# Visiting order and block sums of 32 experts: from GpSimd on one partition to TensorE and VectorE on 32 partitions

## The reference

```
logits = (tok @ w_router) + b_router           # 288 tokens x 32 experts
top_val, top_idx = lax.top_k(logits, 4)
gate = softmax(top_val)
counts = bincount(flat_e, length=32)           # tokens of each expert
...
hid = xb @ w_e_in[e] + b_e_in[e]               # 1024 x 2048 per expert, float32
act = x_glu * sigmoid(1.702 * x_glu) * (x_lin + 1.0)
out = act @ w_e_out[e] + b_e_out[e]            # 1024 x 1024 per expert, float32
y = sum over a token's 4 experts of gate * out
x = layer_norm(alpha * x + g2 * y, ...)
```

## Time and profile before

| | us |
|---|---|
| median of 3 runs | 1367.17 (1365.32 to 1367.57) |
| the profiled execution | 1369.23 |
| its span, first to last instruction | 1367.5 |
| PE busy | 1095.1 (80%) |
| DVE busy | 509.9 (37%) |
| ACT busy | 173.9 (13%) |
| POOL busy | 84.1 (6%) |
| mean rate of the DMA engines | 334 GB/s |

### The profile page before, as it was taken

One profiled execution on the slowest core, in us unless ns is written; L12 is line 12 of the kernel. 1 busy time (PEld: TensorE's weight loads), 2 busy tenths in 40 slices (PEclk: granted clock), 3 DMA queues, 4 the chain that ended last, 5 costly groups with the idle time before them and its releaser, 6 DMA issues.

```text
span 1367.5 us, 31578 instructions
## 1 busy us (share of the span) xinstructions
PE 1095.1 (80%) x12593; PEld 488.9 (36%) x12594; DVE 509.9 (37%) x1154; ACT 173.9 (13%) x506; POOL 84.1 (6%) x118
## 2 busy tenths in 40 slices
PE   3789888859889999899997997797987887666760
PEld 2556544424324433343433433242423332222210
DVE  0393323854324333243433333233323322222228
ACT  0101222221111111111111111010101100000000
POOL 2700000072000000000000000000000000000003
PEclk9899756969989999899999999898988987878765
DMA  9985851355991798969798999999999999999980
GB/s 327 326 306 193 271 196 62 129 214 214 415 417 61 309 418 335 412 268 418 324 416 323 417 416 416 415 417 417 417 417 417 416 416 416 415 418 417 417 319 35
DMA packets 94555, 457.15 MB, mean 334 GB/s; under 512 B 9163, under 2 KB 16245, under 8 KB 61633
## 3 DMA queue, kind: packets, MB, share of 16 engines
q1 hardware_dynamic: 89984, 450.18, 82.4%
q10 hardware_dynamic: 4481, 5.59, 1.3%
HBM read 452.51 MB, written 3.79 MB: 334 GB/s over the span
## 4 chain that ended last, share of the span: by engine, by line
PE 36%; SPq 30%; DMA 17%; DVE 8%; issue 5%; DVEq 2%; ACT 1%; ACTq 0%; POOL 0%
SPq L373 15%; DMA w<-in_w_e_out 13%; PE bank L1612 13%; SPq L370 9%; PE bank L1639 4%; PE bank L1592 3%; SPq L351 2%; DMA w<-in_w_e_in 2%; PE comb L1571 2%; PE bank L1509 2%; DMA mt<-in_ln_b 1%; SPq L337 1%; DMA w<-in_w_ada 1%; PE comb L1421 1%; PE comb L1418 1%
## 5 line engine op out<-in xcount | busy, mean ns | idle before, releaser
L1612 PE MATMUL bank<-w,mt 128*32 128x512 f32 x3264 | 405.7, 640 | 51.8 <-DMA w<-in_w_e_in 51.8
L1178 DVE TENSOR_TENSOR xy<-comb,xy 128x1024 f32<-128x1024 f32 x156 | 185.2, 1215 | 243.7 <-PE comb L1571 243.7
L1639 PE MATMUL bank<-w,mt 128*32 128x256 f32 x3264 | 204.9, 397 | 49.8 <-DMA w<-in_w_e_out 36.2
L1612 PEld LDWEIGHTS bank<-w,mt 128*32 128x32 f32 x3264 | 96.2, 114 | 320.1 <-issue 207.8
L1215 DVE TENSOR_SCALAR mt<-bank 128x256 f32<-128x256 f32 x51 | 21.6, 424 | 404.9 <-PE bank L1612 404.9
L1639 PEld LDWEIGHTS bank<-w,mt 128*32 128x32 f32 x3264 | 100.7, 113 | 135.7 <-DMA w<-in_w_e_out 53.4
L1592 PE MATMUL bank<-pick,hb 128*128 128x32 bf16 x2448 | 79.4, 179 | 62.3 <-issue 38.2
L1571 PE MATMUL comb<-mt,gpickT 32*128 32x256 f32 (+1 forms) x1248 | 115.9, 456 | 1.9 <-DVE xy L1178 1.4
L1592 PEld LDWEIGHTS bank<-pick,hb 128*128 128x128 bf16 x2448 | 75.1, 98 | 87.4 <-issue 87.4
L803 ACT ACTIVATE mt<-mt 128x256 f32<-128x256 f32 x51 | 21.2, 416 | 513.8 <-DVE mt L1215 513.8
L1593 PE MATMUL bank<-pick,hb 96*128 96x32 bf16 x408 | 72.6, 179 | 0.0
(11 more groups left out here) (320 smaller groups left out, 847.2 us busy)
## 6 DMA issues: line engine op xcount, KB each, us to landing
w<-in_w_e_in SPq DMA_DIRECT2D x256, 1024.0 KB, 20.7
w<-in_w_e_out SPq DMA_DIRECT2D x128, 1024.0 KB, 21.8
w<-in_w_ada SPq DMA_DIRECT2D x12, 2048.0 KB, 11.1
w<-in_w_in SPq DMA_DIRECT2D x3, 2048.0 KB, 22.0
w<-in_w_in SPq DMA_DIRECT2D x2, 1024.0 KB, 21.3
w<-in_w_out SPq DMA_DIRECT2D x4, 512.0 KB, 10.2
w<-in_w_out SPq DMA_DIRECT2D x2, 1024.0 KB, 12.8
w<-mod_rows SPq DMA_DIRECT2D x4, 512.0 KB, 6.4
```

Source lines behind the costliest of these rows:

```text
L1178: return v.tensor_tensor(rows, comb[0:TS[t], :, c:c + 256], rows, ALU.add)
L1612: ins = mm(quarter(bank[0][SLOTS * q:SLOTS * (q + 1), :], 0), xT[:, SLOTS * k:SLOTS * (k + 1)], quarter(slot[s], q), start=False, stop=(k ...
L1639: ins = mm(bank[7][SLOTS * q:SLOTS * (q + 1), 0:256], hid, slot[s][:, D * (k % 2) + 256 * q:D * (k % 2) + 256 * (q + 1)], start=False, sto ...
```

## The change

- PE forms the counts twice, as a column with one expert per partition (`maskb` against a column of ones) and as a row on all 32 partitions (ones against `maskb`), after the ranks instead of before them.
- DVE compares all pairs of experts in one instruction on 32 partitions, with a key of count times 32 plus a tie-breaker, sums each row to a rank, and compares the rank with a constant table `rank_at` of which rank stands at which place. The result `at_place` is a permutation matrix, and `upto` is its running sum along the places.
- PE multiplies the expert numbers with `at_place` and the numbers of blocks with `upto`, in two small matmuls. That gives `order` and the whole of `cum`. DVE copies both to SBUF after the gates, and each copy counts `cum_ready` up by one.
- The constants (`tie`, `tiec`, `rank_at`, `idb`) are written by POOL early in the kernel, ahead of the splitting of the expert biases (L501 to L510). POOL's own work L524 to L562 is gone.
- The rank's two subtractions of 1 (L1159, L1162) are gone; `iota` starts at 1 and `rank` is cleared to 0 in their place.
- PE, ACT and DVE no longer load range ends before expert 0. They enter its loop with 0 and a register that is loaded inside the loop, in each of its blocks: PE behind the last matmul of L1612, ACT behind its second copy of gathered tokens, DVE behind `add_y(0)`. The same place loads expert 1's end.
- SP waits for both copies of `cum_ready` at L415; all waits for `order_ready` are gone.

```
         def opening_range(eng, name):
             return [0] + [eng.alloc_register(f"{name}_end{e}") for e in range(2)]
         def load_ends(eng, ends):
             eng.wait_ge(cum_ready, 2)
             for e in range(2):
                 eng.reg_load(ends[e + 1], cum[0:1, e + 3:e + 4])
...
+            g.iota(idb[:, 0:1], ...)
+            g.iota(tie[:, :], ...)
+            link(g.iota(tiec[:, :], ...))
+            for e, first in ((0, 1e6), (1, 9e5)):
+                link(g.memset(tie[:, e:e + 1], first))
+                link(g.affine_select(out=tiec[:, :], ...))
+            for place, r in enumerate(PLACES):
+                g.memset(rank_at[:, place:place + 1], float(r))
+            link(g.memset(cum[:, 0:3], 0))
+            g.sem_inc(sort_consts, 1)
...
-            dve.wait_ge(cnt_done, 1)                 # DVE L1143 to L1154
-            ... counts, blocks, nblk_ready, cumf, cum, three register loads
             dve.wait_ge(rank_done, 1)
             ... ranks without the two subtractions
+            dve.wait_ge(cnt_done, 1)
+            dve.wait_ge(sort_consts, 1)
+            link(v.tensor_copy(cntc[:, 0:1], bank[7][0:NE, 288:289]))
+            v.scalar_tensor_tensor(out=keyr, in0=bank[7][0:NE, 256:288], scalar=float(NE), in1=tie, op0=MULT, op1=ADD)
+            v.tensor_scalar(over, full, cntc[:, 0:1], None, ALU.is_le)
+            link(v.scalar_tensor_tensor(out=cntc[:, 1:2], in0=cntc[:, 0:1], scalar=float(NE), in1=tiec, ...))
+            link(v.tensor_scalar(keyr, keyr, cntc[:, 1:2], None, ALU.is_gt))
+            v.tensor_reduce(idb[:, 1:2], over, AX_X, ALU.add)
+            link(v.tensor_reduce(cntc[:, 2:3], keyr, AX_X, ALU.add))
+            v.tensor_scalar(idb[:, 1:2], idb[:, 1:2], 1.0, None, ALU.add).then_inc(place_ready, 1)
+            link(v.tensor_scalar(at_place, rank_at, cntc[:, 2:3], None, ALU.is_equal))
+            v.tensor_tensor_scan(upto, at_place, at_place, 0.0, ALU.add, ALU.max).then_inc(place_ready, 1)
             ... gates, seven semaphore increments
+            dve.wait_ge(order_done, 1)
+            v.tensor_copy(cum[:, 3:NE + 3], bank[7][0:1, 352:384]).then_inc(cum_ready, 1)
+            v.tensor_copy(order[:, :], bank[7][0:1, 320:352]).then_inc(cum_ready, 1)
...
+            for t in range(3):                       # PE, behind the ranks
+                mm(bank[7][0:NE, 288:289], maskb[0:TS[t], t, :], ones[0:TS[t], 0:1], ...)
+            for t in range(3):
+                ins = mm(bank[7][0:NE, 256:288], ones[0:TS[t], 0:NE], maskb[0:TS[t], t, :], ...)
+            ins.then_inc(cnt_done, 1)
+            pe.wait_ge(place_ready, 2)
+            mm(bank[7][0:1, 320:352], idb[:, 0:1], at_place[:, :], start=True, stop=True)
+            mm(bank[7][0:1, 352:384], idb[:, 1:2], upto[:, :], start=True, stop=True).then_inc(order_done, 1)
...
-            pe.wait_ge(cum_ready, 1)
...
                     ins.then_inc(m["U"], 1)          # PE, inside the block loop
+                    if isinstance(e, int) and e == 0:
+                        load_ends(pe, ends)
```

More of the change, by code:

```diff
@@ L283, in block_range, with opening_range, load_ends @@
             return lo, hi
+        PLACES = [0, 1] + [31 - (p - 2) // 2 if p % 2 == 0 else 2 + (p - 3) // 2 for p in range(2, NE)]
+        def opening_range(eng, name):
+            return [0] + [eng.alloc_register(f"{name}_end{e}") for e in range(2)]
+        def load_ends(eng, ends):
+            eng.wait_ge(cum_ready, 2)
+            for e in range(2):
+                eng.reg_load(ends[e + 1], cum[0:1, e + 3:e + 4])
         def expert_at(eng, e):
@@ L522, in _ @@
                 g.memset(XY[:, ORD[i], :], 0.0).then_inc(y_zero, 1)
[L524 to L556, removed]
-            link(g.tensor_tensor(grid, across(place), down(ids), ALU.subtract))
-            link(g.tensor_scalar(grid, grid, 0.0, None, ALU.is_le))
-            link(g.tensor_tensor(grid, grid, across(cnt[0:1, 1, :]), ALU.mult))
-            fold(heavy)
-            link(g.tensor_copy(cum[0:1, 5:NE + 3], heavy[:, 2:NE]))
-            g.sem_inc(order_ready, 1)
             pool.wait_ge(ld_x1, 5 * 16)
@@ L1149, in _ @@
-            link(v.tensor_scalar(cnt[0:1, 1, :], cnt[0:1, 1, :], 1.0, None, ALU.add))
-            dve.sem_inc(nblk_ready, 1)
-            link(v.tensor_tensor_scan(cumf[0:1, 3:5], cnt[0:1, 1, 0:2], cnt[0:1, 1, 0:2], 0.0, ALU.add, ALU.max))
-            v.tensor_copy(cum[:, 0:5], cumf[:, 0:5]).then_inc(cum_ready, 1)
-            dve.wait_ge(cum_ready, 1)
-            opening = [block_range(dve, e) for e in range(2)]
             dve.wait_ge(rank_done, 1)
-            link(v.scalar_tensor_tensor(out=rank[:, 0:2, :], in0=bank[1][:, 128:128 + 2 * NE].rearrange("p (t e) -> p t e", t=2), scalar=1.0,
-                                        in1=maskf[:, 0:2, :], op0=ALU.add, op1=ALU.mult))
@@ new lines, in _ @@
+            v.tensor_scalar(over[:, :], full, cntc[:, 0:1], None, ALU.is_le)
+            link(v.scalar_tensor_tensor(out=cntc[:, 1:2], in0=cntc[:, 0:1], scalar=float(NE), in1=tiec[:, :], op0=ALU.mult, op1=ALU.add))
+            link(v.tensor_scalar(keyr[:, :], keyr[:, :], cntc[:, 1:2], None, ALU.is_gt))
+            v.tensor_reduce(idb[:, 1:2], over[:, :], AX_X, ALU.add)
+            link(v.tensor_reduce(cntc[:, 2:3], keyr[:, :], AX_X, ALU.add))
+            v.tensor_scalar(idb[:, 1:2], idb[:, 1:2], 1.0, None, ALU.add).then_inc(place_ready, 1)
@@ L1165, in _ @@
+            link(v.tensor_scalar(at_place[:, :], rank_at[:, :], cntc[:, 2:3], None, ALU.is_equal))
+            v.tensor_tensor_scan(upto[:, :], at_place[:, :], at_place[:, :], 0.0, ALU.add, ALU.max).then_inc(place_ready, 1)
             dve.wait_ge(gexp_done, 3)
@@ L1547, in _ @@
             for t in range(3):
-                ins = mm(bank[2][0:1, 0:NE], ones[0:TS[t], 0:1], maskb[0:TS[t], t, :], start=(t == 0), stop=(t == 2))
-            ins.then_inc(cnt_done, 1)
-            for t in range(3):
                 n = TS[t]
```

64 lines of the change are left out of this document (36 added, 28 removed).

## The result

The changed kernel takes 1360.01 us in the median of 20 runs (1351.88 to 1366.14), the kernel before, timed beside it, 1367.80 us (1362.53 to 1373.56, 20 runs). The ratio is 0.9944 [0.9929, 0.9958]: 7.7 us faster, with 5.7 to 9.7 inside the interval. The forecast was 9.1 us and 1358.1 us; both it and the 6.7 us of rival 1 lie inside the interval, so the times alone can't tell the two apart, and the profiles have to.

The account below looks back on a forecast made before the run. DMA of the experts' weights bounds the kernel, chained to SP's issue at 322.65. 4.3 + 2.66 + 2.42 - 0.3 = 9.1 us off the 1367.17 median gives 1358.1 us, range 1355.0 to 1364.5.

Parts of the forecast that it names:

- rival 1: TensorE's clock falls in the first block's gap all the same: 6.7 us gained, 1360.5 us; chance 0.12.
- A: DVE's path up to expert 0's first block: PE starts at 290.2 instead of 294.47, 4.3 us gained (2.8 to 4.9).
- B: Activation of expert 0's first block, without POOL's work beside it: 2.66 us gained, at least 2.4.
- C: Second product (L1639) of expert 0's first block, at full clock as in the second block: 2.42 us gained (0 to 2.42).
- D: Clock at PE's start, again low after the pause: 0.3 us lost, between 0 and 0.9.
- E: Register loads inside expert 0's loop, hidden behind other work: nothing lost, upper bound 0.8 us.
- F: Work moved and added elsewhere, POOL's early constants and the waits: nothing reaches PE; 2 us if the cover were gone.
- rival 3: PE's jump back misses its code, up to 6.9 us each; chance 0.02 for one, 0.04 for two or more.
- Rival 4: Clock stays low through expert 0: 10.4 us lost against 7.0 gained, 1370.6 us; chance 0.02.
- rival 2: The lead is absorbed where DMA is full in the last third: time stays at 1367; chance 0.07.
- the chain to SP's first issue: Everything after SP's issue at 322.65 is chained to it; a shift there should reach the end one to one.
- The landmark: SP's issue of expert 1's last pieces, at 322.65 before, forecast at 313.5.

Follow-up runs that it names:

- e9: c0 plus 14 dead two-input POOL instructions of 1x1024 from the gather of expert 0's first block on; 1368.95 us in a single execution.
- e1: c0 with POOL's old sort put back as dead work, started once DVE has the numbers of blocks; 1364.89 us (12 runs), ratio to before 0.999.
- e2: c0 with POOL's old sort as dead work, released only after the gather of the first block's tokens; 1358.57 us in a single execution.
- e10: c0 plus ten dead one-input POOL instructions of 1x1024 from the gather of the first block on; 1362.57 us in a single execution.
- e4: c0 plus one dead DVE reduction inside the activation in both blocks of expert 0, POOL silent; 1368.74 us in a single execution.
- e3: c0 with both range ends loaded ahead of expert 0's loop on PE, ACT and DVE; 1367.75 us in a single execution.
- e5: c0 plus 22 dead DVE multiplications, about 10 us, in front of the gates; 1370.65 us (12 runs), ratio to before 1.0031.
- e7: c0 with POOL's three clears of XY moved behind the first block's pick; 1357.70 us (12 runs), ratio to before 0.9923.
- e6: c0 plus 12 dead matmuls of 512 columns while PE waits for DVE before the first block; 0.3 us won to SP's issue.
- e8: e7 plus seven increments moved to POOL, the copies of the sums to ACT, and 19 dead matmuls on PE; 1355.80 us (6 runs), ratio to before 0.9913.
- c0: The changed kernel with each range end loaded with stated bounds, then moved to its register; 1360.58 us (12 runs), ratio to before 0.9955.

## Why the prediction was right

**A, DVE's path (4.3 us, between 2.8 and 4.9): 4.5.** The ten operations took 1.67 us, below my lower bound of 1.7 (2.1 taken): start to start they are 0.16, not 0.21. L1154 took the 0.26 assumed, the two copies 0.59 from start to end (0.35 taken), since 0.22 us of issue lies between them. I missed one thing upstream: `choose` for the last tile took 0.95 us longer in after, because of how L1099 met POOL's clears. In this pair its `lg` began 0.61 earlier, by luck, which hid most of it: measured from the mask, the way to PE shrank by 4.84, and 4.84 - 0.95 + 0.61 = 4.50. So the 4.5 agrees with the 4.3 in part by luck; DVE's path itself beat the sum, mostly in the ten operations (0.5 less) and the gates (0.2 less). The best end, 4.9, is 0.2 more than its terms give: 2.1 less 1.7 is 0.4.

**B, the activation (2.66, at least 2.4): 2.66.** All 51 of these instructions are now alike, where the longest was 2177:

```profile
L1208 DVE SCALAR_TENSOR_TENSOR mt<-mt x51: 425/426/427, 301.7 to 1301.4; 128x256 f32<-128x256 f32 x51
```

Cause shown by e9 and by e1's L1198; e2 shows that the same sort at another time leaves this activation untouched.

**C, the clock in the second product (2.42): 2.42.** Rival 1 is wrong for the first block's gap of 2.77 us; in the same place e10 lost 1.7 us at 3.47, e4 and e9 2.3 and 2.6 at 5.3 to 5.6, so the step stood on 0.7 us at most, which I had not seen. It also stood on a weaker argument than it looked. I took the second block, whose gap of 2.77 left the clock at full, as the model of the first; e4 shows that the second block kept its full clock even behind a gap of 5.30 us, so its rows said little about the first. And TensorE did not stand still for most of the gap before, but for 2.7 of 5.6 us. The result was as forecast; this reason for it was not enough.

**D, the low clock at PE's start (-0.3): -0.18.** It lasted a little over 4 us, as before.

**E, the register loads in the loop (0, at most 0.8): 0.** The line of the loads in the changed kernel, by engine (ns min/median/max, first and last start; all four loads of the two blocks):

```profile
L298 ACTq TENSOR_LOAD <-cum x4: 277/285/478, 291.7 to 309.1; - x4
L298 DVEq TENSOR_LOAD <-cum x4: 305/322/540, 292.9 to 309.8; - x4
L298 PEldq TENSOR_LOAD <-cum x4: 305/312/483, 298.0 to 314.3; - x4
```

PE's sequencer began at 298.0, 2.7 us before the array was through with L1605 (300.69). e3 shows what the move was worth: 1.8 us on the path for two loads, where the prediction removed 2.19 before L1157 for three.

**F, elsewhere (0): 0**, as far as the medians can tell. The five stalls at the jumps back over five experts are all there (6.8 to 7.6 us, at 542.72, 733.76, 864.22, 1029.02 and 1165.97) and no new one of that size, so rival 3 fell; the row of the first, against the earlier trace rows:

```profile
542.72 0.32 PE L1585 MATMUL bank<-pick,hb 128*128 128x32 bf16 x6 [6.98 <-issue]
```

Rival 4 fell with the stretches above (1.00 from 294.5 on), rival 2 with e5. One reading of the page was off: slice 13 of the DMA engines, given as near full, stands at 1. TensorE was busy for 33.0 of the 34 us from 410 to 444 there, so it is work and not a late stream that makes this dip, and the chain to SP's first issue holds.

**The size.** The landmark moved by the 9.1 forecast (9.4 in the pair, 8.8 in the sum of stretches), and the medians by 7.7 with an interval that holds both (and rival 1's 6.7). Where I was too sure was the runs: I took their spread as 2 us from three of them, and it is 11 to 14 over 20.

## What to carry to other kernels

A helper engine that is itself off the critical path can still be paid for there: look at the duration of the same instruction in its other repetitions (median against maximum) before asking whether the helper's work is late. Stretching a gap of a few microseconds in TensorE's work can cost nearly as much again in the clock behind it, and a gap that was safe in one block need not be in another (e4), so the granted clock is worth reading at the very place. In a stream bound by DMA, read a small change at the event that starts the stream, relative to an event ahead of the change; single times of such a kernel say little.

## What was not expected of the hardware

- Beside a POOL instruction with two inputs (1x1024, 1.9 us) a two-input DVE instruction waits to its end, and ends 0.29 us (128x256) or 0.12 us (128x96) after it. Beside a one-input POOL instruction of 2.76 us it was held for 0.7 us, and the next one not at all (e10).
- A DVE `tensor_scalar` of 128x32 took 2.52 us beside three POOL clears of 128x1024 and ended with the last of them (280.13 and 280.10), where it takes 0.23 alone (e7). Before, the same clears were met by three such instructions, at 0.74, 0.89 and 0.41.
- 12 dead matmuls ahead of the first block left its gather at the lower clock (e6); in e8, with 19 and fewer pauses, the clock was at the upper from the gather on, worth 1.5 us to SP against c0, where e6 won 0.3.
- In one and the same kernel (e4) a gap of 5.55 us cost the clock of the product behind it and the next block's gap of 5.30 us did not, while in e10 a gap of 3.47 us with TensorE busy for 2.34 of it did.
